# The memory heads of a two-layer mixer: gate blocks as weights, denominators in a value column, seven gate projections in the tail

## The reference

```python
log_intra = jnp.where(causal, cum_f[..., :, None] - cum_f[..., None, :] + igc[..., None, :], -jnp.inf)
m = jnp.maximum(log_inter, jnp.max(log_intra, axis=-1))
scores = jnp.einsum('bhtd,bhsd->bhts', qc, kc) * jnp.exp(log_intra - m[..., None])
num = scores @ vc + w_inter[..., None] * (qc @ c_prev)
h_out = num / jnp.maximum(jnp.abs(den), jnp.exp(-m))[..., None]
...
hh = _rms_norm(hh, out_gain)            # over the 128 of a head
y_ml = sigmoid(o_pre) * hh
...
g = sigmoid(gates)                      # three blocks of 1024 columns
merged = g[0] * (y_sb @ w_up_sb) + g[1] * (y_ml @ w_up_ml) + g[2] * (y_mla @ w_up_mla)
x = x + merged @ w_out
```

## Time and profile before

| what | value |
|---|---|
| median of 3 runs | 2614.5 us (2613.51 to 2614.93) |
| profiled execution | 2616.07 us |
| its span, first to last instruction | 2613.2 us |
| TensorE, VectorE, ScalarE, GpSimd busy | 97%, 55%, 36%, 38% |
| mean granted TensorE clock | 0.993 |
| mixers: values to last merged block | about 1000 to 1493 us, and 1890 to 2388 us |
| gated-memory heads | 1290 to 1330 and 1395 to 1432 us; 2290 to 2328 us for the second pair of layer 1 |

### The profile page before, as it was taken

How to read it: one execution, slowest core, us unless ns; L and a number is a source line. 1 busy time by engine, 2 the same in 40 slices (tenths; PEclk the granted TensorE clock), 3 DMA queues, 4 the chain that set the end, 5 groups by cost and what they waited for, 6 DMA issues and landing times.

```text
span 2613.2 us, 27821 instructions
## 1 busy us (share of the span) xinstructions
PE 2543.1 (97%) x11166; PEld 1992.8 (76%) x11166; DVE 1434.5 (55%) x1937; ACT 947.5 (36%) x1429; POOL 992.1 (38%) x432
## 2 busy tenths in 40 slices
PE   7999999999999999998999999999999989999999
PEld 7777767888888888676676788888887666867887
DVE  5768667644325632369645854344324886278441
ACT  4444443322223223545324432332335453254321
POOL 3423224444444444234232444444432342424443
PEclk9999999999999999999999999999999999999999
DMA  4211122333333333122121233233321211313233
GB/s 172 73 33 57 49 64 90 97 93 95 95 97 107 97 92 101 49 65 65 49 73 57 89 95 98 90 97 97 97 87 49 65 57 49 96 50 95 92 97 96
DMA packets 59600, 213.29 MB, mean 82 GB/s; under 512 B 6608, under 2 KB 6736, under 8 KB 59344
## 3 DMA queue, kind: packets, MB, share of 16 engines
q1 hardware_dynamic: 59472, 211.52, 26.5%
HBM read 209.39 MB, written 2.10 MB: 81 GB/s over the span
## 4 chain that ended last, share of the span: by engine, by line
PE 82%; DVE 13%; issue 2%; ACT 1%; POOL 1%; DMA 0%; DVEq 0%; SPq 0%; ACTq 0%; POOLq 0%
PE banks L652 81%; DVE t L1475 1%; DVE t L1472 1%; DVE t L1357 1%; DVE t L1000 1%; DVE t L1092 1%; DVE t L1002 1%; DVE t L1098 1%; DVE t L1477 1%; DVE t L998 1%; POOL t L1758 1%; DVE t L1195 1%; DVE t L1399 1%; DVE t L1353 0%; PE banks L761 0%
## 5 line engine op out<-in xcount | busy, mean ns | idle before, releaser
L652 PE MATMUL banks<-t,t 128*128 128x512 f32 (+7 forms) x10854 | 2511.9, 394 | 54.2 <-POOL t L1758 30.5
L652 PEld LDWEIGHTS banks<-t,t 128*128 128x128 f32 (+3 forms) x10854 | 1958.1, 189 | 576.7 <-issue 104.0
L1758 POOL TENSOR_TENSOR t<-t,t 128x1024 fp32r<-128x1024 f32 x387 | 936.2, 2419 | 1540.9 <-ACT t L1517 1540.9
L1517 ACT ACTIVATE t<-t 128x1024 fp32r<-128x1024 f32 x387 | 409.3, 1058 | 1197.1 <-PE banks L652 1194.9
L1092 DVE TENSOR_TENSOR t<-banks,t 128x512 f32<-128x512 f32 x121 | 83.0, 687 | 211.7 <-PE banks L652 211.4
L982 DVE SCALAR_TENSOR_TENSOR t<-t,t,t 128x512 fp32r<-128x512 f32 x64 | 113.7, 1776 | 62.5 <-ACT t L1526 62.5
L1252 DVE TENSOR_TENSOR t<-banks,t 128x512 f32<-128x512 f32 x44 | 30.4, 691 | 180.7 <-PE banks L652 180.4
L1195 DVE CAST t<-t 128x512 fp32r<-128x512 f32 x68 | 114.3, 1681 | 2.5
L1220 DVE SCALAR_TENSOR_TENSOR t<-banks,t 128x512 f32<-128x512 f32 x32 | 22.1, 692 | 158.0 <-PE banks L652 158.0
L1239 DVE CAST t<-t 128x512 fp32r<-128x512 f32 x32 | 67.7, 2115 | 30.5 <-ACT t L1632 30.5
L998 DVE SCALAR_TENSOR_TENSOR t<-banks,t 128x512 f32<-128x512 f32 x53 | 36.4, 686 | 74.9 <-ACT t L1540 74.8
(11 more groups left out here) (147 smaller groups left out, 1310.7 us busy)
## 6 DMA issues: line engine op xcount, KB each, us to landing
t<-in_w SPq DMA_DIRECT2D x387, 512.0 KB, 3.6
t<-in_xT SPq DMA_DIRECT2D x8, 256.0 KB, 6.3
out<-t SPq DMA_DIRECT2D x8, 256.0 KB, 4.3
t<-in_dmask SPq DMA_DIRECT2D x1, 1536.0 KB, 11.8
t<-in_vbias SPq DMA_DIRECT2D x2, 384.0 KB, 3.9
t<-in_c SPq DMA_DIRECT2D x1, 576.0 KB, 8.5
t<-in_pos SPq DMA_DIRECT2D x2, 256.0 KB, 6.2
t<-in_smask SPq DMA_DIRECT2D x1, 256.0 KB, 12.0
```

Of the source, the lines that this page charges most:

```text
L652: return pe.matmul(o, l, r, start=start, stop=stop, skip_group_check=True)
L1517: a.activation(whl[u % 2][:, 0:1024], wraw[u % 3][:, :], ACT.Copy).then_inc(*w_high.next(u))
L1758: p.tensor_tensor(hl[:, 1024:2048], wraw[u % 3][:, :], as_f32(hl[:, 0:1024]), ALU.subtract).then_inc(*w_low.next(u))
```

## The change

Each ml head is computed with the operands exchanged. The gate block (128 keys by 128 positions) is the weight and the values of a key block move: for each of the four blocks of positions the key blocks up to it are summed, ten matmuls (`ml_y`). The values have a 129th column of ones, so that the same matmul gives the denominators as a column beside the output, whose rows are now positions. What was done on 512 columns for denominators, floor and normalisation is done on four columns (`ml_den`, `ml_mean`, `ml_root`, `ml_factor`), ScalarE sums squares while squaring (`ml_squares`), and the factor is applied per row. `ml_turn` then turns the four blocks back. `ml_floor`, the product with ones and `ml_sum` are gone; the floor comes as a column from `fgate_out`, which turns FM too and so waits for it. The diagonal's mask is now a minimum before the exponent, in `ml_e`, on 128 columns.

The output-gate projections follow gate projection 16, write into the tiles of scored queries and keys, and seven gate projections (17 to 23) follow them. The first three heads now run before the output gates, the fourth beside those seven. The eight conversions are items (`half2`) of their own, each put when its source is there. The merging takes the branches in the order sb, mla, ml. A few tiles lie elsewhere, and 2 KB more are used.

```diff
-        for g in range(20):
+        for g in range(MLO_AT):
             full("gt", "w_in_2", l, K8, W2["gate"] + 128 * g)
         for t in range(4):
             full("mlo", "w_in_2", l, K8, W2["mlo"] + 128 * t)
-        for g in range(20, 24):
+        for g in range(MLO_AT, 24):
             full("gt", "w_in_2", l, K8, W2["gate"] + 128 * g)
         for m in range(8):
             full("us", "w_up_sb_2", l, range(2), 128 * m)
+            full("ua", "w_up_mla_2", l, range(2), 128 * m)
...
-        LVt = reg(64, 4 * S)[:, :].rearrange("p (u c n) -> p u c n", u=4, c=4)
+        LVt = reg(64, 16 * 129)[:, :].rearrange("p (u c n) -> p u c n", u=4, c=4)
+        MLS = [[small_t[:, o + 4 * k:o + 4 * k + 4] for k in range(6)] for o in (64, 88)]
+        MLO = [LQ[0], LK[0], LQ[1], LK[1]]
...
             def fgate_out(l, slot):
                 bk = pair(slot)[0]
-                need.wait_ge(*v_attn.at(("fgate_a", l)))
+                need.wait_ge(*v_attn.at(("fgate_f", l)))
                 free(bk)
-                for c in range(4):
-                    ins = pe.transpose(B[bk][:, 4 * c:4 * c + 4], ar[:, 128 * c:128 * c + 128], C["ident"][0:4, 0:4])
+                for k, row in enumerate((ar, FM)):
+                    for c in range(4):
+                        ins = pe.transpose(B[bk][:, 16 * k + 4 * c:16 * k + 4 * c + 4], row[:, 128 * c:128 * c + 128],
+                                           C["ident"][0:4, 0:4])
                 ins.then_inc(*t_attn.next(("fgate", l)))
                 bank[bk] = [(v_attn, ("acol", l))]
...
+            def ml_y(l, h):
...
+                for b in range(4):
+                    bk, o = pair(slot)[b // 2], 129 * (b % 2)
+                    if b % 2 == 0:
+                        free(bk)
...
+                    for j in range(b + 1):
+                        need.wait_ge(*v_attn.at(("ml_g", l, h, j)))
+                        ins = mm(B[bk][:, o:o + 129], MLG[i][1][j][:, 128 * (b - j):128 * (b - j) + 128], LVt[:, h, j, :],
+                                 j == 0, j == b)
+                ins.then_inc(*t_attn.next(("ml_y", l, h)))
+            def ml_turn(l, h):
+                need.wait_ge(*v_attn.at(("ml_yn", l, h)))
...
+                for b in range(4):
+                    ins = pe.transpose(B[ba][:, 128 * b:128 * b + 128], MLG[i][0][:, 128 * b:128 * b + 128], C["ident"])
+                ins.then_inc(*t_attn.next(("ml_turn", l, h)))
...
+            def ml_e(l, h):
...
+                Mc, gp = MLG[i]
                 need.wait_ge(*t_attn.at(("ml_m", l, h)))
...
+                v.tensor_copy(Mc, B[pair(slot)[0]]).then_inc(*v_attn.next(("ml_m", l, h)))
...
+                for j in range(4):
+                    v.scalar_tensor_tensor(out=gp[j][:, 0:128], in0=Mc[:, 128 * j:128 * j + 128],
+                                           scalar=acol[:, 4 * j + h:4 * j + h + 1], in1=C["m01i"], op0=A_,
+                                           op1=MN).then_inc(*v_attn.next(("ml_e", l, h, j)))
             def ml_gate(l, h, j):
...
+            def ml_blocks(l, h, k):
+                return B[pair(ml_at[l, h][0])[k]][:, 0:258].rearrange("p (b n) -> p b n", n=129)
+            def ml_den(l, h):
+                d4, inv = MLS[ml_at[l, h][1]][0:2]
+                floor = fcol.rearrange("p (c h) -> p c h", h=4)[:, :, h]
...
+                need.wait_ge(*a_attn.at(("fcol", l)))
+                for k in range(2):
+                    den, o = ml_blocks(l, h, k)[:, :, 128], d4[:, 2 * k:2 * k + 2]
+                    v.scalar_tensor_tensor(out=o, in0=den, scalar=-1.0, in1=floor[:, 2 * k:2 * k + 2], op0=M_,
+                                           op1=MX).then_inc(*v_attn.next())
...
+                    v.tensor_tensor(o, den, o, MX).then_inc(*v_attn.next(("ml_den", l, h)))
...
+                v.reciprocal(inv, d4).then_inc(*v_attn.next(("ml_inv", l, h)))
...
+                v.tensor_tensor(d4, inv, inv, M_).then_inc(*v_attn.next(("ml_inv2", l, h)))
+            def ml_mean(l, h):
...
+                v.tensor_tensor(ss, ss, d4, M_).then_inc(*v_attn.next(("ml_mean", l, h)))
+            def ml_factor(l, h):
...
+                d4, inv, ss, y, u, f = MLS[i]
...
+                v.tensor_tensor(u, y, y, M_).then_inc(*v_attn.next())
+                v.tensor_tensor(f, y, inv, M_).then_inc(*v_attn.next())
...
+                v.scalar_tensor_tensor(out=u, in0=ss, scalar=128 * EPS, in1=u, op0=A_, op1=M_).then_inc(*v_attn.next())
...
+                v.tensor_scalar(u, u, -0.5 / 128, 1.5, M_, A_).then_inc(*v_attn.next())
...
+                v.tensor_tensor(f, f, u, M_).then_inc(*v_attn.next())
...
+                for b in range(4):
+                    v.tensor_scalar(MLG[i][0][:, 128 * b:128 * b + 128], ml_blocks(l, h, b // 2)[:, b % 2, 0:128],
+                                    f[:, b:b + 1], None, M_).then_inc(*v_attn.next())
+                v_attn.table["ml_yn", l, h] = v_attn.n
             def ml_open(l, h):
...
+                need.wait_ge(*t_attn.at(("ml_turn", l, h)))
...
+                reach(need, *branch[l]["cq_read"])
+                v.scalar_tensor_tensor(out=YL[h], in0=B[pair(ml_at[l, h][0])[0]], scalar=col(f"on_{l}", h), in1=MLO[h],
+                                       op0=M_, op1=M_).then_inc(*v_attn.next(("ml_open", l, h)))
...
             def merge2(l, m, gs, tl, bz):
-                for i in range(3):
+                for i, of in enumerate((0, 2, 1)):
...
-                    need.wait_ge(*a_evac.at(("open2", l, 8 * i + m)))
+                    need.wait_ge(*a_evac.at(("open2", l, 8 * of + m)))
...
+            def ml_e(l, h):
+                Mc, gp = MLG[ml_at[l, h][1]]
...
+                for j in range(4):
+                    need.wait_ge(*v_attn.at(("ml_e", l, h, j)))
+                    a.activation(gp[j][:, 0:128], gp[j][:, 0:128], ACT.Exp).then_inc(*a_attn.next(("ml_e", l, h, j)))
+                    if j < 3:
+                        a.activation(gp[j][:, 128:S - 128 * j], Mc[:, 128 * j + 128:S], ACT.Exp,
+                                     bias=acol[:, 4 * j + h:4 * j + h + 1]).then_inc(*a_attn.next(("ml_e", l, h, j)))
+            def ml_squares(l, h):
+                slot, i, after = ml_at[l, h]
+                need.wait_ge(*v_attn.at(("ml_den", l, h)))
+                for b in range(4):
+                    y = B[pair(slot)[b // 2]][:, 129 * (b % 2):129 * (b % 2) + 128]
+                    a.activation(MLG[i][0][:, 128 * b:128 * b + 128], y, ACT.Square,
+                                 accum_out=MLS[i][2][:, b:b + 1]).then_inc(*a_attn.next(("ml_ss", l, h)))
...
                 def gen(slot):
...
+                    yield "t", *ya_all, (a_attn, ("silu", l, h)), *ml_slot.get(slot, ())
                     while not ml_free:
...
+                        yield "t", (t_attn, ("ml_turn", l, h - 2))
                     i, after = ml_free.pop(0)
...
+                    ml_slot[slot] = ((v_attn, ("ml_open", l, h)),)
                     put("ml_m", l, h)
...
+                    yield "va", (t_attn, ("ml_m", l, h))
+                    put("ml_e", l, h)
                     for j in range(4):
...
+                        yield "t", (v_attn, ("ml_g", l, h, j - 2) if j > 1 else ("ml_m", l, h))
                         put("ml_z", l, h, j)
...
                         yield "v", (a_attn, ("ml_e", l, h, j)), (t_attn, ("ml_scores", l, h, j))
                         put("ml_gate", l, h, j)
+                    sch.done.add(("mlz", l, h))
                     yield "t", (v_attn, ("ml_g", l, h, 3))
...
+                    put("ml_y", l, h)
+                    yield "v", (t_attn, ("ml_y", l, h))
                     put("ml_den", l, h)
...
+                    yield "a", (v_attn, ("ml_den", l, h))
+                    put("ml_squares", l, h)
+                    yield "v", (a_attn, ("ml_ss", l, h))
+                    put("ml_mean", l, h)
+                    put("ml_root", l, h)
+                    yield "v", (a_attn, ("ml_root", l, h))
+                    put("ml_factor", l, h)
+                    yield "t", (v_attn, ("ml_yn", l, h))
+                    put("ml_turn", l, h)
+                    ml_free.append((i, ((t_attn, ("ml_turn", l, h)),) + ya_all))
+                    yield "v", (t_attn, ("ml_turn", l, h)), (a_evac, ("mlo", l, h))
                     put("ml_open", l, h)
...
                 return gen
...
-            for g_ in range(14, 20):
+            for g_ in range(14, MLO_AT):
                 gt[g_] = proj("gt", s, GT[GATE2[g_]], ya_all)
-            r = [proj("mlo", s, GT[GATE2[20 + t_]], ya_all, bcol(l, "mlo", t_)) for t_ in range(4)]
+            sch.until(("mlz", l, 0), ("mlz", l, 1))
+            scored = tuple((t_attn, ("ml_scores", l, h_, 3)) for h_ in range(2))
+            r = [proj("mlo", s, MLO[t_], scored, bcol(l, "mlo", t_)) for t_ in range(4)]
             for t_ in range(4):
                 put("mlo", l, t_, r[t_])
-                sch.done.add(("mlo", l, t_))
             put("explog")
```

(20 more changed lines are left out.)

187 lines of the change are left out of this document (62 added, 125 removed).

## The result

| | before | after |
|---|---|---|
| median | 2614.0 us (2613.2 to 2614.9, 4 runs) | 2593.4 us (2591.3 to 2594.1, 4 runs) |
| ratio, 95% interval | | 0.992 (0.9902 to 0.9937) |
| span of the profiled execution | 2613.2 us | 2590.9 us |

What follows compares the result with a forecast made beforehand. TensorE, busy 97%, was taken as the bound, so removed work and closed gaps count. From 2616.07 us profiled, -48.8 + 23.2 + 4.6 - 14.5 - 5.9 + 5.0 = -36.4 gave 2579.7, median 2578, range 2567 to 2595.

Steps and rivals of the forecast that it cites:

- Points 1 and 2: TensorE work in the eight ml heads: 6.10 us removed per head (-48.8 us), 2.9 us added per head (+23.2 us).
- Point 3: Gate's turn, now waiting for FM: +4.6 us over two layers; the reordered rest of that stretch costed at 0, +-2.
- Point 4: Mixers' ends: seven gate projections behind the output gates remove 14.5 us of gaps and 5.9 us of low clock.
- Point 5: New waits inside heads, 1.5 us per layer; with 1.0 for the fourth head's row maximum, +5.0 us in all.
- Point 6: Memset, strided value writes, split reciprocal and merge order costed at nothing; the end of the merging stays as it is.
- B: New values product's weight loads partly in the open, 4.8 us a product: +19, 2597 us; chance 0.10.
- D: New values product runs wholly serial, 9.5 us each: +57, 2635 us, slower than before; chance 0.03.
- C: Heads' chains late, each of eight turns delayed 2.4 us by a GpSimd collision: 2595 us; chance 0.14.
- E: Work goes, but equal gaps return elsewhere (reordered stretch, end of merging): 2598 us; chance 0.07.
- A: The forecast itself: 2578 us, own range 2568 to 2588; chance 0.66.

Runs made afterwards that it cites:

- experiment 2: experiment 1's kernel, with TensorE really waiting for FM before the gate's turn, unknown to the planner, so the order stays: 2573.3 us.
- experiment 1: The changed kernel with FM turned, copied and exponentiated in its own step at the first memory head, restoring the earlier order up to the heads: 2566.4 us.
- experiment 6: experiment 1's kernel with the output-gate projections behind gate 19, so four gate projections follow them instead of seven: 2569.1 us.
- Experiment 8: experiment 1's kernel with each output gate's sigmoid right behind its own projection instead of all four behind the last: 2564.3 us.
- experiment 5: The kernel before with only the small tile widened from 64 to 112 columns, moving all later tiles 192 bytes: 2606.6 us.
- experiment 7: experiment 1's kernel with the ten matmuls of every new values product issued twice: 2580.6 us.

## Why the prediction was right, and where not

- Points 1 and 2 (work removed and added) hold. The product costs 2.27 to 2.4 us as forecast, the turn 0.49. TensorE's busy time fell by 30.4 us; the forecast's terms make -48.8 + 23.2 + 0.8 - 5.9 = -30.7. That these agree is chance: the measured figure holds some 13 us of half clock in the reordered stretch and 7.8 us of gain from the layout, neither of which was forecast.
- Point 3 failed, in the sentence "the rest of that stretch is in another order (the planner), but the same work ... I cost it at 0, +-2". The wait itself was near (2.48 us against 1.9 + 0.5), and with its clock worth 3.5 us per layer on average in experiment 2 against 2.3 forecast. The order was worth some 20 us: it put the third latent projection behind the stick-breaking products, and with it came the 5.6 us wait for L1001 and the half clock. Same work in another order isn't the same time where VectorE's slow operations have to fit: by experiment 1 the whole point costs 27 us instead of 4.6.
- Point 4: the gaps went, all of them. The reason given, seven gates behind the output gates, was only a small part of it (experiment 6). The clock did not come back whole: at the mixers' ends 6.8 us in each layer were at half clock before, and 3.4 us in each still are, now right behind the row maximum's wait (granted clock 0.70 from 1390 to 1395 us and from 2274 to 2279). That gives back some 3.4 us, where 5.9 were forecast.
- Point 5: 1.16 us for the row maximum and 0.95 us for turns per layer, 2.1 against the 2.5 forecast. Experiment 8 shows the next wait standing right behind.
- Point 6, costed at nothing, held a gain of 7.8 us for the position of the tiles (experiment 5), of which 3.8 are seen before the first mixer. "A few tiles lie elsewhere" was not weighed at all. It explains about half of the 8 us by which the heads and the tail beat the forecast. TensorE's waits there fell by 11.0 us (17.8 to 6.8) against 9.5 forecast, and the clock gave 2.5 us less than forecast, so by this count an estimated 5 us lie in the work of the heads. Which product was worth more than forecast was not taken apart.
- Rivals: B and D are excluded by the product's pitch and experiment 7, C by turns that wait 0.8 us at most. E is what happened beside A: its 2598 us assumed 20 us coming back in the reordered stretch, and 27 came back, of which the layout hid 8. At 0.07 it was held too unlikely.
- The range held in part by luck. The prediction names a sign of being wrong, "gaps over 3 us stand in the reordered stretch (E)", and two of 5.6 and 5.7 us do. Point 3 cost some 22 us more than forecast by experiment 1; the 7.8 us from the layout, which nobody had weighed, took part of it off. Without them the time would be near 2601 us, outside the range of 2567 to 2595.

## What to carry to other kernels

Where a planner makes the order, each wait that an edit adds or moves reorders everything behind it, and the price is that of the new order: read both orders for the engine with long operations, and if a result isn't needed soon, fetch it in a step of its own (here the floors, needed 200 us later, 27 us). If a wait comes back elsewhere when its instruction is moved, look at what feeds the engine waited for, and when. And change a tile's size alone once: a gain or loss from positions alone is otherwise taken for that of the edit.

## What the runs showed of the hardware

- The pace of TensorE's blocks in part of the stages goes by where the tiles lie: 5.60, 5.49, 5.60 and 5.44 us with all later tiles 0, 192, 256 and 384 bytes further. The same instructions took 2614.4 and 2606.6 us at 0 and 192 bytes, and those of experiment 8 took 2564.3, 2571.6 and 2554.5 us at 192, 256 and 384. Which operand makes it wasn't tried.
- A wait of 1.2 to 5.7 us was often followed by a stretch at the 1.2 GHz level, even though TensorE was then busy throughout (clock 0.51 from 1155 to 1160 us after the wait for L1001). Not always: behind the same wait of the fourth head's row maximum the clock was 0.66 from 1378 to 1383 us in experiment 1 and 1.00 from 1380 to 1395 in experiment 7.
- Two low-half steps of VectorE took 1.41 us at 1122.95, with no split of GpSimd beside them, and 3.54 us at 1139.82, with the split of 1140.01 to 1142.81 beside them.
- Ten fp32 matmuls with a new 128x128 block of weights each and 129 columns moving (1290 columns) take 2.27 us by the pitch of the splits and 2.4 by the records. The old product, 1280 columns in four matmuls, took 2.17 by the pitch. So the ten loads of weights cost at most 0.1 to 0.2 us beside them.
